# First mixer's attentions: the sign and scale folded into the queries, the two maps mixed by one operation, the output scaled on its way out of its bank by ScalarE

## The chip, the cores and the metric

The kernel runs on one core of a Trainium2 chip. The metric is the device time of one execution in microseconds (us); lower is better. All matrix products named below are in f32.

## What is computed

The whole program is two stacks of two layers on 512 tokens of width 1024. Only the first mixer of the first stack matters here. It has two attentions: A with 4 heads, each with two maps over 64-wide queries and keys and 128-wide values, and B with 8 heads of 96-wide queries and keys and 64-wide values. Cut to what is touched:

```
# attention A (diff_attention), per head and block of 128 queries
s = einsum('bhmqd,bhmkd->bhmqk', qb, k) * scale          # m = 0, 1
p = softmax(s, axis=-1)
w = p[:, :, 0] - lam * p[:, :, 1]
o = einsum('bhqk,bhke->bhqe', w, v)
...
# attention B (latent_attention), per head and block
s = (einsum(qn, k_nope) + einsum(qr, k_rope)) * scale
o = einsum('bhqk,bhke->bhqe', softmax(s), v)
```

A's output goes through an RMS norm over each head's 128 columns, and both outputs through one output projection.

## The kernel before

Each engine has its own program, and semaphores order them. `attention(name)` exists once for TensorE (PE), once for ScalarE (ACT) and once for VectorE (DVE). Each loops over blocks i of 128 queries: 16 blocks in A (4 groups, one a head, of 4 blocks) and 32 in B (8 groups). The engines are skewed against each other by whole blocks:

- PE in step i: the score products s(i) (line 1921; two maps in A, one in B), in step 2 of each group also the eight transposes that turn the next group's queries and keys (line 1906), then the four transposes t(i-2) of the exponentials (line 1936), then the four output products o(i-3) (line 1945). It goes through them in this order.
- DVE in step i: for each map a row maximum of the scores straight from the bank (line 2779) and a small product with minus the scale (line 2781), which releases the exponential; then for block i-1 the reciprocal of the sums (line 2788), in A the mixing of the two maps by two operations (lines 2792 and 2795), which releases t(i-1); then the copy of o(i-3) out of its bank (line 2805 in A, line 2808 in B, where it is also scaled by the reciprocal).
- ACT in step i: for each map the exponential with its accumulated row sum (line 1244, two records: the activation and the reading of the accumulator); in step 2 of each group the two copies of turned queries and keys out of their banks (line 1226); then the copy of the turned exponentials t(i-2) (line 1255), which releases o(i-2).

Banks of PSUM are handed out in a fixed rotation over eight, four a block in A (two scores, one t, one o), and a bank is taken again when its last reader has reported. In B's steps 6 and 10 on ACT and 8 and 12 on DVE a chunk of the output projection's weights is rounded and split (lines 1236 and 2773), in line with the attention's work. `keep_warm` issues idle products before stages in which PE would otherwise wait.

After B come the sums of squares over A's output on DVE (lines 3236 and 3238), a reciprocal root on POOL, the norm, the output projection, the layer norm, routing and 32 experts with streamed weights, and the rest of the program.

Of the kernel before, what the change touches and what calls it, by code (L numbers as in the profile page):

```python
# [7 lines left out]
ALU = mybir.AluOpType  # L8
ACT = mybir.ActivationFunctionType
# [4 lines left out]
AX_X = mybir.AxisListType.X  # L14
# [4 lines left out]
T = S // P  # L19
# [166 lines left out]
def build(nc, a, out, stages=99):  # L186
    table, where = shape_constants()
    ctx = ExitStack()
    with ctx:
# [40 lines left out]
        full = [sem(f"bank{i}_full") for i in range(N_BANKS)]  # L230
        drained = [sem(f"bank{i}_drained") for i in range(N_BANKS)]
# [5 lines left out]
        dve_done = Signal(sem("dve_done"))  # L237
# [4 lines left out]
        def signal(name):  # L242
            if name not in sig:
                sig[name] = Signal(sem(name))
            return sig[name]
# [11 lines left out]
        def ps(u):  # L257
            return psum[u.bank]
# [3 lines left out]
        U, W = {}, {}  # L262
# [227 lines left out]
        for i in range(4):  # L490
            c = plan.chunk(KD, BANK, BANK)
# [176 lines left out]
        sums, negmax, rcp = stat(64), stat(64), stat(64)  # L668
        bnst, mv, rstd = stat(T, 2, 6), stat(T, 2), stat(32)
        ssq = stat(32)  # L670
        lam = stat(8)
# [73 lines left out]
        def on(n):  # L745
# [8 lines left out]
                      v=lambda g, o, kt: E["H"][:, kt, 2 * A_QKV + 128 * g:2 * A_QKV + 128 * g + 128],  # L754
                      o=lambda g, o, t: XH[:, t, 128 * g:128 * g + 128]),
            "B": dict(groups=B_HEADS, maps=1, outs=1, rows=B_QK, scale=B_QK ** -0.5, buf=E, dv=B_V,
                      q=lambda g, t: E["QB"][:, t, g, :], k=lambda g, t: E["KC"][:, t, g, :], width=B_QK,
                      v=lambda g, o, kt: E["VB"][:, kt, g, :],
                      o=lambda g, o, t: XH[:, t, 512 + B_V * g:512 + B_V * g + B_V]),
# [310 lines left out]
        def _(act):  # L1070
# [146 lines left out]
            def attention(name, then=None):  # L1217

                c = att[name]
                u, buf, n = U[name], att[name]["buf"], att[name]["groups"] * T  # L1220

                def group(g):
                    for j in range(2):
                        v = u["qk"][g][j]
                        act.wait_ge(full[v.bank], v.n + 1)
                        act.activation(buf["QKT"][0:c["width"], g % 2, j, :], ps(v)[0:c["width"], :], ACT.Copy).then_inc(
                            drained[v.bank], 1)
                        act.wait_ge(drained[v.bank], v.n + 1)

                group(0)  # L1230
                for i in range(n + 2):
                    if then and i in (6, 10):
                        first = W[then][0]
                        ks = pieces(first)[i // 10]
                        act.wait_ge(loaded[first.slot], 16 * first.loads)
                        act.activation(one_pass(hi(first)[:, ks, :]), raw(first)[:, ks, :], ACT.Copy).then_inc(rounded[first.pair], 1)
                    if i < n:
                        for m in range(c["maps"]):
                            s = i * c["maps"] + m
                            act.wait_ge(signal("max_ready").sem, signal("max_ready").next(act))  # L1240
                            v = u["s"][i][m]
                            j = s % 64
                            act.wait_ge(full[v.bank], v.n + 1)
                            act.activation(buf["p"][i % 3][:, m, :], ps(v)[:, :], ACT.Exp, bias=negmax[:, j:j + 1], scale=c["scale"], accum_out=sums[:, j:j + 1]).then_inc(
                                drained[v.bank], 1)
                            act.wait_ge(drained[v.bank], v.n + 1)
                        if i % T == 2 and i // T + 1 < c["groups"]:
                            group(i // T + 1)
                    if i >= 2:
                        for o in range(c["outs"]):  # L1250
                            if i >= 4:
                                act.wait_ge(full[u["o"][i - 4][o].bank], u["o"][i - 4][o].n + 1)
                            v = u["t"][i - 2][o]
                            act.wait_ge(full[v.bank], v.n + 1)
                            act.activation(buf["WT"][:, (i - 2) % 2, o, :, :].rearrange("p t q -> p (t q)"), ps(v)[:, :], ACT.Copy).then_inc(
                                drained[v.bank], 1)
                            act.wait_ge(drained[v.bank], v.n + 1)
# [123 lines left out]
            n = n_dma = 0  # L1381
            for name in chan_at:
                v = a[name]
                v = v.rearrange("(r c) -> r c", c=P) if len(v.shape) == 1 else (
                    v.rearrange("l (r c) -> (l r) c", c=P) if len(v.shape) == 2 else v.rearrange("l w (r c) -> (l w r) c", c=P))
# [11 lines left out]
            for name in bc_at:  # L1397
                v = a[name]
                if len(v.shape) == 2:
                    v = v.rearrange("a b -> (a b)")  # L1400
# [30 lines left out]
            for t in range(T):  # L1431
                for j in range(2):
                    u = U["uq"][0][2 * t + j]
# [1206 lines left out]
        def _(dve):  # L2640
# [122 lines left out]
            def attention(name, then=None):  # L2763
                c = att[name]
                u, buf, n = U[name], c["buf"], c["groups"] * T

                for i in range(n + 3):
                    g, t = divmod(i, T)
                    if then and i in (8, 12):
                        first = W[then][0]  # L2770
                        ks, w = pieces(first)[i // 12], raw(first)
                        dve.wait_ge(rounded[first.pair], 2 * first.nth - 1 + i // 12)
                        dve.tensor_tensor(one_pass(w[:, ks, :]), w[:, ks, :], parts(hi(first)[:, ks, :]), ALU.subtract).then_inc(split[first.pair], 1)
                    if i < n:
                        for m in range(c["maps"]):
                            s = (i * c["maps"] + m) % 64
                            v = u["s"][i][m]
                            dve.wait_ge(full[v.bank], v.n + 1)
                            dve.tensor_reduce(negmax[:, s:s + 1], ps(v)[:, :], AX_X, ALU.max).then_inc(dve_done.sem, 1)  # L2779
                            dve.wait_ge(dve_done.sem, dve_done.next(dve))  # L2780
                            dve.tensor_scalar(negmax[:, s:s + 1], negmax[:, s:s + 1], -c["scale"], None, ALU.mult).then_inc(
                                signal("max_ready").sem, 1)
                            dve.wait_ge(signal("max_ready").sem, signal("max_ready").next(dve))
                    if 1 <= i <= n:
                        s = ((i - 1) * c["maps"]) % 64
                        for m in range(c["maps"]):
                            dve.wait_ge(drained[u["s"][i - 1][m].bank], u["s"][i - 1][m].n + 1)
                        dve.reciprocal(rcp[:, s:s + c["maps"]], sums[:, s:s + c["maps"]]).then_inc(dve_done.sem, 1)
                        dve.wait_ge(dve_done.sem, dve_done.next(dve))
                        if name == "A":  # L2790
                            p0, p1 = (buf["p"][(i - 1) % 3][:, m, :] for m in range(2))
                            dve.tensor_scalar(p1, p1, rcp[:, s + 1:s + 2], lam[:, 2:3], ALU.mult, ALU.mult).then_inc(
                                dve_done.sem, 1)
                            dve.wait_ge(dve_done.sem, dve_done.next(dve))
                            dve.scalar_tensor_tensor(p0, p0, rcp[:, s:s + 1], p1, ALU.mult, ALU.add).then_inc(
                                signal("mixed").sem, 1)
                            dve.wait_ge(signal("mixed").sem, signal("mixed").next(dve))
                    if i >= 3:
                        g2, t2 = divmod(i - 3, T)
                        for o in range(c["outs"]):  # L2800
                            v = u["o"][i - 3][o]
                            s = ((i - 3) * c["maps"] + o) % 64
                            dve.wait_ge(full[v.bank], v.n + 1)
                            if name == "A":
                                dve.tensor_copy(c["o"](g2, o, t2), ps(v)[:, 0:c["dv"]]).then_inc(drained[v.bank], 1)
                                dve.wait_ge(drained[v.bank], v.n + 1)
                            else:
                                dve.tensor_scalar(c["o"](g2, o, t2), ps(v)[:, 0:c["dv"]], rcp[:, s:s + 1], None, ALU.mult).then_inc(
                                    drained[v.bank], 1)
                                dve.wait_ge(drained[v.bank], v.n + 1)  # L2810

            def shifted(j):

# [416 lines left out]
            if on(2):  # L3230
                attention("A")
                attention("B", "even_o")

                o = XH[:, :, 0:512]
                sq = E["H"][:, :, 0:512]
                dve.tensor_tensor(sq, o, o, ALU.mult).then_inc(dve_done.sem, 1)
# [482 lines left out]
```

## Time and profile before

| what | value |
|---|---|
| time, median of 3 runs | 3312.08 us (3310.1 to 3312.66) |
| span of the profiled execution | 3301.4 us |
| busy over the span: PE, PEld, DVE, ACT, POOL | 95%, 72%, 66%, 48%, 13% |
| attention A in the profiled execution | about 150 to 215 us |
| attention B | about 215 to 307 us |

The span runs from the first to the last instruction; the time of a run takes in what lies around it. The profiled execution's own time is not among those given; its span lies 10.7 us under the median of the timed runs, and those three lie within 2.6 us of each other.

### The profile page before, as it was taken

The numbers are of one execution on the slowest core, as the hardware profiler recorded it, in microseconds if no ns is written. First come the engines' busy times: TensorE is split into PE (matmuls) and PEld (weight loads), VectorE is DVE, ScalarE is ACT, GpSimd is POOL, SyncE is SP. The second block draws the span as 40 slices with busy tenths as digits, with TensorE's granted clock in tenths as the row PEclk, the third lists the DMA queues.
The fourth block names the chain that finished last, engine by engine and source line by source line (L and its number), as shares of the span: only waits on it lengthen the run. The fifth ranks groups of instructions, "written<-read, shape, count | busy, mean of one in ns | idle before, by whom it ended". The sixth has DMA issues, their size and how long they took to land.

```text
span 3301.4 us, 39275 instructions
## 1 busy us (share of the span) xinstructions
PE 3133.6 (95%) x14815; PEld 2391.1 (72%) x14815; DVE 2171.0 (66%) x2380; ACT 1594.0 (48%) x1889; POOL 415.7 (13%) x274
## 2 busy tenths in 40 slices
PE   8879999999998989899999999998899999999998
PEld 7556667777776867577777757877788887788886
DVE  2375578888885266688888876564477745757653
ACT  2465167777774344477777754342322212722211
POOL 0000122222212000222223220010000000000000
PEclk9999999999999999999999999999999999999999
DMA  7200389999993211699999973330123223223321
GB/s 263 106 1 14 149 309 361 351 358 360 359 355 134 77 46 65 249 363 348 356 361 351 360 279 73 76 65 1 60 94 98 82 101 102 77 83 102 102 102 64
DMA packets 174479, 599.20 MB, mean 181 GB/s; under 512 B 25571, under 2 KB 74899, under 8 KB 124947
## 3 DMA queue, kind: packets, MB, share of 16 engines
q1 hardware_dynamic: 140528, 541.75, 44.9%
q0 software_dynamic: 23472, 51.42, 4.4%
q10 hardware_dynamic: 10355, 4.33, 0.5%
q8 instruction: 83, 1.36, 0.2%
q14 instruction: 41, 0.34, 0.0%
HBM read 581.17 MB, written 48.23 MB: 191 GB/s over the span
## 4 chain that ended last, share of the span: by engine, by line
PE 78%; DVE 8%; DMA 6%; ACT 4%; issue 3%; POOL 1%; DVEq 0%; SPq 0%; ACTq 0%; POOLq 0%
PE bank L1820 20%; PE bank L1822 19%; PE bank L1821 19%; DMA ring<-w_gate 3%; PE bank L1832 3%; PE bank L2368 2%; PE bank L1884 2%; PE bank L1885 2%; PE bank L2118 1%; PE bank L1827 1%; PE bank L1828 1%; DVE st L2779 1%; PE bank L1945 1%; ACT ring_rounded L1276 1%; PE bank L2149 1%
## 5 line engine op out<-in xcount | busy, mean ns | idle before, releaser
L1821 PE MATMUL bank<-ring_rounded,big_rounded 128*96 128x512 f32 (+1 forms) x1680 | 660.1, 393 | 0.0
L3019 DVE TENSOR_TENSOR ring_rounded<-ring,big_rounded 128x2048 fp32r<-128x2048 f32 x252 | 568.1, 2287 | 42.2 <-ACT big_rounded L1276 41.3
L2666 DVE TENSOR_TENSOR ring_rounded<-ring,ring_rounded 128x2048 fp32r<-128x2048 f32 (+2 forms) x124 | 273.4, 2247 | 402.0 <-ACT ring_rounded L1096 401.9
L1276 ACT ACTIVATE big_rounded<-ring 128x2048 fp32r<-128x2048 f32 x252 | 478.6, 1918 | 74.2 <-DMA ring<-w_up 56.6
L1096 ACT ACTIVATE ring_rounded<-ring 128x2048 fp32r<-128x2048 f32 (+2 forms) x124 | 226.7, 1878 | 454.9 <-DMA ring<-ffn_w_down 163.6
L1820 PE MATMUL bank<-big_rounded 128*96 128x512 f32 x992 | 395.0, 398 | 1.0 <-DVE ring_rounded L3019 0.8
L3019 DVE TENSOR_TENSOR ring_rounded<-ring,ring_rounded 128x2048 fp32r<-128x2048 f32 x128 | 292.6, 2287 | 156.4 <-ACT ring_rounded L1276 148.1
L1822 PE MATMUL bank<-big_rounded,XH_rounded 128*96 128x512 f32 x992 | 392.1, 395 | 0.0
L1821 PEld LDWEIGHTS bank<-ring_rounded,big_rounded 128*96 128x96 f32 (+1 forms) x1680 | 277.5, 165 | 105.4
L1276 ACT ACTIVATE ring_rounded<-ring 128x2048 fp32r<-128x2048 f32 x128 | 245.1, 1916 | 208.3 <-DMA ring<-w_gate 208.0
L1822 PE MATMUL bank<-ring_rounded,XH_rounded 128*96 128x512 f32 (+1 forms) x776 | 307.2, 396 | 0.0
L1820 PE MATMUL bank<-ring_rounded,big_rounded 128*96 128x512 f32 (+1 forms) x688 | 276.2, 401 | 11.8 <-DVE XH_rounded L3028 4.9
L1820 PE MATMUL bank<-XT_rounded,ring_rounded 128*128 128x512 f32 x696 | 274.1, 394 | 2.4 <-DVE big L3108 2.4
L1821 PE MATMUL bank<-XH_rounded,ring_rounded 128*128 128x512 f32 x696 | 271.6, 390 | 0.0
L1822 PE MATMUL bank<-XT_rounded,ring_rounded 128*128 128x512 f32 x696 | 271.4, 390 | 0.0
L1820 PE MATMUL bank<-ring_rounded,XT_rounded 128*128 128x512 f32 (+1 forms) x584 | 228.7, 392 | 9.4 <-DVE XH_rounded L3450 3.9
L1822 PE MATMUL bank<-ring_rounded,big_rounded 128*128 128x512 f32 (+1 forms) x608 | 235.7, 388 | 0.0
L956 POOL DMA_INDIRECT expert_rows<-big,idx x64 | 118.2, 1847 | 865.8 <-ACT big L1298 809.3
L1821 PE MATMUL bank<-ring_rounded,XT_rounded 128*128 128x512 f32 (+1 forms) x584 | 227.0, 389 | 0.0
L1822 PEld LDWEIGHTS bank<-big_rounded,XH_rounded 128*96 128x96 f32 x992 | 159.8, 161 | 70.3
L1820 PEld LDWEIGHTS bank<-big_rounded 128*96 128x96 f32 x992 | 162.2, 164 | 66.9 <-DVE ring_rounded L3019 1.7
L905 POOL TENSOR_SCALAR st<-st 128x1 f32<-128x1 f32 (+3 forms) x43 | 16.4, 382 | 1523.0 <-ACT lnp L1355 918.6
(464 smaller groups left out, 5238.1 us busy)
## 6 DMA issues: line engine op xcount, KB each, us to landing
ring<-w_up SPq DMA_DIRECT2D x128, 1024.0 KB, 7.6
ring<-w_down SPq DMA_DIRECT2D x128, 1024.0 KB, 7.8
ring<-w_gate SPq DMA_DIRECT2D x128, 1024.0 KB, 7.0
ring<-ffn_w_up SPq DMA_DIRECT2D x44, 1024.0 KB, 6.9
ring<-ffn_w_down SPq DMA_DIRECT2D x10, 2048.0 KB, 7.8
ring<-ret_gdn_w_in SPq DMA_DIRECT2D x8, 2048.0 KB, 13.3
expert_rows<-lnp POOLq DMA_DIRECT2D x1, 12288.0 KB, 40.2
ring<-odd_w_qkv SPq DMA_DIRECT2D x6, 2048.0 KB, 8.0
```

Of the source, the lines that this page charges most:

```text
L956: pool.indirect_dma_start(expert_rows, bass.IndirectOffsetOnAxis(ap=used[0:CAP, e:e + 1], axis=0), M["YE"][0:CAP, e % 2, :], None, bounds_ ...
L1096: act.activation(one_pass(hi(c)[:, ks, :]), raw(c)[:, ks, :], ACT.Copy).then_inc(rounded[c.pair], 1)
L1276: act.activation(one_pass(expert_hi(j)), expert_raw(j), ACT.Copy).then_inc(signal("half_rounded").sem, 1)
L1820: pe.matmul(dst, x_hi, y_hi, start=first, stop=False)
L1821: pe.matmul(dst, x_hi, y_lo, start=False, stop=False)
L1822: return pe.matmul(dst, x_lo, y_hi, start=False, stop=last)
L1832: return pe.matmul(dst, one_pass(x_hi), one_pass(y_lo), start=False, stop=last)
L1884: pe.matmul(dst, w, one_pass(XT[:, kk, :].rearrange("p (t c) -> p t c", t=T)), start=(kk == 0), stop=False)
L1885: pe.matmul(dst, w, x_lo, start=False, stop=False)
L2368: ins = pe.matmul(ps(u)[:, tokens(h)], lhsT[:, h, :], rhs[:, h, :], start=start and (stop or h == 0), stop=stop and (start or h == GDN_HEA ...
L2666: dve.tensor_tensor(one_pass(w), w, parts(hi(c)[:, ks, :]), ALU.subtract).then_inc(split[c.pair], 1)
L3019: dve.tensor_tensor(one_pass(expert_raw(j)), expert_raw(j), parts(expert_hi(j)), ALU.subtract).then_inc(signal("half_split").sem, 1)
```

## The change

Four edits, all in the first mixer's attentions:

1. ACT's copy of the turned queries multiplies by minus the scale (`scale=-c["scale"]` as a constant), so that the scores in the bank are already negated and scaled. DVE takes their minimum, which is what the exponential needs as its bias, and the small product of line 2781 goes. The exponential takes the constant -1 as its scale.
2. In A the two maps are mixed as e0 + (lam · sum0 / sum1) · e1: a small product on one column makes the factor, and one operation over 512 columns remains where there were two.
3. The missing factor 1/sum0 is put on A's output, as it is copied out of its bank.
4. That copy moves from DVE to ACT, `out(i)`, at the head of ACT's step i+4, ahead of that step's exponentials; ACT's loop in A has two steps more at its end. Ahead of the sums of squares DVE waits for the last four of these copies.

```diff
@@ ACT, attention
-  act.activation(buf["QKT"][...], ps(v)[...], ACT.Copy)
+  act.activation(buf["QKT"][...], ps(v)[...], ACT.Copy, scale=1.0 if j else -c["scale"])
...
+  def out(i):
+      v = u["o"][i][0]
+      act.wait_ge(full[v.bank], v.n + 1)
+      s = i * c["maps"] % 64
+      act.activation(c["o"](i // T, 0, i % T), ps(v)[:, 0:c["dv"]], ACT.Copy, scale=rcp[:, s:s + 1]).then_inc(drained[v.bank], 1)
...
-  for i in range(n + 2):
+  for i in range(n + (4 if name == "A" else 2)):
+      if name == "A" and i >= 4:
+          out(i - 4)
...
-  act.activation(buf["p"]..., ACT.Exp, bias=negmax[:, j:j + 1], scale=c["scale"], accum_out=sums[:, j:j + 1])
+  act.activation(buf["p"]..., ACT.Exp, bias=negmax[:, j:j + 1], scale=-1.0, accum_out=sums[:, j:j + 1])
...
-  if i >= 2:
+  if 2 <= i < n + 2:
@@ DVE, attention
-  dve.tensor_reduce(negmax[:, s:s + 1], ps(v)[:, :], AX_X, ALU.max)
-  dve.tensor_scalar(negmax[:, s:s + 1], negmax[:, s:s + 1], -c["scale"], None, ALU.mult)
+  dve.tensor_reduce(negmax[:, s:s + 1], ps(v)[:, :], AX_X, ALU.min)
...
-  dve.tensor_scalar(p1, p1, rcp[:, s + 1:s + 2], lam[:, 2:3], ALU.mult, ALU.mult)
-  dve.scalar_tensor_tensor(p0, p0, rcp[:, s:s + 1], p1, ALU.mult, ALU.add)
+  dve.tensor_scalar(rcp[:, s + 1:s + 2], rcp[:, s + 1:s + 2], sums[:, s:s + 1], lam[:, 2:3], ALU.mult, ALU.mult)
+  dve.scalar_tensor_tensor(p0, p1, rcp[:, s + 1:s + 2], p0, ALU.mult, ALU.add)
...
-  if i >= 3:
+  if i >= 3 and name == "B":
-      dve.tensor_copy(c["o"](g2, o, t2), ps(v)[:, 0:c["dv"]])        # A's
@@ DVE, after the attentions
+  for v in U["A"]["o"][-4:]:
+      dve.wait_ge(drained[v[0].bank], v[0].n + 1)
```

## Rows read from the trace of the kernel before

**Rows 1.** The page: the chain that ended last, by engine, as shares of the span.
```profile
PE 78%; DVE 8%; DMA 6%; ACT 4%; issue 3%; POOL 1%; DVEq 0%; SPq 0%; ACTq 0%; POOLq 0%
```

**Rows 2.** Busy time by stretch: length, busy PE, PEld, DVE, ACT, POOL, granted clock, DMA.
```profile
150.00:216.00 66.00, 51.93 (x288) 33.80 (x288) 55.06 (x128) 38.15 (x87) 0.00 (x0) 0.90 0.00 1
216.00:307.00 91.00, 82.03 (x508) 61.34 (x506) 45.60 (x130) 56.98 (x114) 0.00 (x0) 0.98 0.00 1
...
180.00:195.00 15.00, 11.98 (x75) 7.54 (x73) 13.51 (x32) 9.81 (x22) 0.00 (x0) 1.00 0.00 1
```

**Rows 3.** The timeline of one block of A on DVE, and the next block's start.
```profile
195.30 0.69 DVE L2779 TENSOR_REDUCE st<-bank 128x1 f32<-128x512 f32 x1
196.02 0.15 DVE L2781 TENSOR_SCALAR st<-st 128x1 f32<-128x1 f32 x1
196.21 0.69 DVE L2779 TENSOR_REDUCE st<-bank 128x1 f32<-128x512 f32 x1
196.26 0.69 ACT L1244 ACTIVATE big<-bank,st 128x512 f32<-128x512 f32 x1 [1.40 <-DVE st L2781]
...
197.32 0.55 DVE L2792 TENSOR_SCALAR ring<-ring,st 128x512 f32<-128x512 f32 x1
197.91 0.75 DVE L2795 SCALAR_TENSOR_TENSOR ring<-ring,st 128x512 f32<-128x512 f32 x1
198.69 0.29 DVE L2805 COPY XH<-bank 128x128 f32<-128x128 f32 x1
199.02 0.69 DVE L2779 TENSOR_REDUCE st<-bank 128x1 f32<-128x512 f32 x1
```

**Rows 4.** The timeline of ACT where it runs without a wait.
```profile
162.73 0.69 ACT L1244 ACTIVATE big<-bank,st 128x512 f32<-128x512 f32 x1
163.54 0.60 ACT L1255 ACTIVATE big<-bank 128x512 f32<-128x512 f32 x1
174.57 1.23 ACT L1226 ACTIVATE big<-bank 128x512 f32<-128x512 f32 x2
```

**Rows 5.** Groups by form, whole span: ScalarE's nearest operations to the new copy.
```profile
L1547 ACT ACTIVATE big<-bank,st 128x128 f32<-128x128 f32 x16 | 4.6, 367 | 0.1
L1517 ACT ACTIVATE big<-bank 128x128 f32<-128x128 f32 x16 | 4.4, 277 | 18.4 <-PE bank L2354 17.9
```

**Rows 6.** The timeline of PE in A; the first and the last row at the low clock.
```profile
149.98 5.49 PE L1921 MATMUL bank<-big 64*128 64x512 f32 x12 [0.98 <-ACT big L1226]
...
161.94 1.16 PE L1945 MATMUL bank<-big 128*128 128x128 f32 x8 [0.52 <-ACT big L1255]
163.03 1.13 PE L1921 MATMUL bank<-big 64*128 64x512 f32 x4
164.15 0.66 PE L1936 MATMUL bank<-const,ring 128*128 128x128 f32 x4
...
165.63 1.13 PE L1921 MATMUL bank<-big 64*128 64x512 f32 x4
...
176.48 1.95 PE L1945 MATMUL bank<-big 128*128 128x128 f32 x8 [0.52 <-ACT big L1255]
```

**Rows 7.** The chain that ended last, start and end of A, in order of time.
```profile
152.13 0.70 DVE st L2779
...
157.35 0.70 DVE st L2779
...
206.46 0.70 DVE st L2779
...
209.06 0.76 DVE ring L2795
...
215.35 0.45 PE bank L1906 x4
```

**Rows 8.** The same chain in one group of B.
```profile
268.05 0.17 DVE st L2781
```

**Rows 9.** The timeline of PE in the same group of B.
```profile
270.99 1.10 PE L1945 MATMUL bank<-lnp,big 128*128 128x64 f32 x8 [0.27 <-ACT big L1255]
```

More of the change, by code:

```diff
@@ L1225, in group @@
                         act.wait_ge(full[v.bank], v.n + 1)
-                        act.activation(buf["QKT"][0:c["width"], g % 2, j, :], ps(v)[0:c["width"], :], ACT.Copy).then_inc(
+                        act.activation(buf["QKT"][0:c["width"], g % 2, j, :], ps(v)[0:c["width"], :], ACT.Copy, scale=1.0 if j else -c["scale"]).then_inc(
                             drained[v.bank], 1)
                         act.wait_ge(drained[v.bank], v.n + 1)
+                def out(i):
[3 more added lines that the diff above has]
+                    act.activation(c["o"](i // T, 0, i % T), ps(v)[:, 0:c["dv"]], ACT.Copy, scale=rcp[:, s:s + 1]).then_inc(drained[v.bank], 1)
                 group(0)
-                for i in range(n + 2):
+                for i in range(n + (4 if name == "A" else 2)):
+                    if name == "A" and i >= 4:
+                        out(i - 4)
                     if then and i in (6, 10):
@@ L1243, in attention @@
                             act.wait_ge(full[v.bank], v.n + 1)
-                            act.activation(buf["p"][i % 3][:, m, :], ps(v)[:, :], ACT.Exp, bias=negmax[:, j:j + 1], scale=c["scale"], accum_out=sums[:, j:j + 1]).then_inc(
+                            act.activation(buf["p"][i % 3][:, m, :], ps(v)[:, :], ACT.Exp, bias=negmax[:, j:j + 1], scale=-1.0, accum_out=sums[:, j:j + 1]).then_inc(
                                 drained[v.bank], 1)
@@ L2778, in attention @@
                             dve.wait_ge(full[v.bank], v.n + 1)
[L2779 to L2782, printed above, removed]
+                            dve.tensor_reduce(negmax[:, s:s + 1], ps(v)[:, :], AX_X, ALU.min).then_inc(signal("max_ready").sem, 1)
                             dve.wait_ge(signal("max_ready").sem, signal("max_ready").next(dve))
@@ L2791, in attention @@
                             p0, p1 = (buf["p"][(i - 1) % 3][:, m, :] for m in range(2))
-                            dve.tensor_scalar(p1, p1, rcp[:, s + 1:s + 2], lam[:, 2:3], ALU.mult, ALU.mult).then_inc(
+                            dve.tensor_scalar(rcp[:, s + 1:s + 2], rcp[:, s + 1:s + 2], sums[:, s:s + 1], lam[:, 2:3], ALU.mult, ALU.mult).then_inc(
                                 dve_done.sem, 1)
                             dve.wait_ge(dve_done.sem, dve_done.next(dve))
-                            dve.scalar_tensor_tensor(p0, p0, rcp[:, s:s + 1], p1, ALU.mult, ALU.add).then_inc(
+                            dve.scalar_tensor_tensor(p0, p1, rcp[:, s + 1:s + 2], p0, ALU.mult, ALU.add).then_inc(
                                 signal("mixed").sem, 1)
                             dve.wait_ge(signal("mixed").sem, signal("mixed").next(dve))
-                    if i >= 3:
+                    if i >= 3 and name == "B":
                         g2, t2 = divmod(i - 3, T)
@@ L2803, in attention @@
                             dve.wait_ge(full[v.bank], v.n + 1)
[L2804 to L2810, printed above, removed]
+                            dve.tensor_scalar(c["o"](g2, o, t2), ps(v)[:, 0:c["dv"]], rcp[:, s:s + 1], None, ALU.mult).then_inc(
+                                drained[v.bank], 1)
+                            dve.wait_ge(drained[v.bank], v.n + 1)
             def shifted(j):
```

## The prediction

> **What bounds the kernel now.** I read the page first. Over the whole program the chain that ended last is PE's for 78% and DVE's for only 8% [rows 1]. A page-wide share says nothing about one stage, so I next read the busy times of the two attentions. In A DVE is busy 55.1 of 66 us, PE 51.9 and ACT 38.2; in B PE is busy 82.0 of 91 us, ACT 57.0 and DVE 45.6 [rows 2]. DMA moves nothing in either, so no transfer can hide or give back what happens there. The timeline of A shows who sets the pace: from one block's first maximum (199.02) back to the one before (195.30) are 3.72 us, in which DVE goes from operation to operation with some 0.03 us between them and waits for nobody, while ACT waits 1.40 us ahead of an exponential for the small product of line 2781 [rows 3]. The chain agrees: through A it is made of DVE's pieces, apart from the start, the end and one stretch near 176 us where PE ran at its low clock, so that its eight output products took 1.95 us in place of 1.16 [rows 6, 7]. In B the chain is mostly PE's, and goes through line 2781 only where a group turns [rows 8] and near the two places where weights are split.
>
> **The change part by part, in A.** A block on DVE costs today: two maxima at 0.69 and two small products at 0.15, the reciprocal, 0.55, 0.75 and 0.29, with the hand-overs 3.72 us [rows 3].
>
> - Line 2781 goes: 196.02 to 196.21 is 0.19 us, twice a block, 0.38.
> - Line 2792 (0.55, with its gap 197.91 - 197.32 = 0.59) becomes a product on one column. Its nearest row is line 2781, 0.19 with the gap; two pointer operands in place of a constant could add a little, below 0.05. Net -0.40.
> - Line 2805 leaves DVE: 199.02 - 198.69 = 0.33.
> - The remaining mixing operation has the form of line 2795 and keeps 0.75; a minimum reads as many elements as a maximum, and a constant scale on a copy or an exponential replaces a constant. I cost these at nothing; nothing hides them, it is the same instruction with another constant. If the minimum were dearer by 0.1, A would lose 0.2 a block on DVE.
>
> DVE's block is then 3.72 - 0.38 - 0.40 - 0.33 = 2.61, say 2.64 us with the pointers.
>
> DVE is then not clearly the slowest, so the other two must be counted. **ACT**: two exponentials at 0.81 start to start and the copy of line 1255 at 0.60 + 0.03 are 2.25 a block; two copies of turned queries and keys, 1.23 + 0.03, come once a group [rows 4]. The new copy is 128x128 from a bank with a pointer as its scale. The trace has that form in another stage: 0.367 us, against 0.277 for one without the pointer [rows 5]. I take 0.37 + 0.03 = 0.40, with 0.30 and 0.45 as bounds. ACT's block is 2.65, and a group 4 × 2.65 + 1.26 = 11.86. **PE** at the full clock: from one s to the next, 163.03 to 165.63, are 2.60 us, of which 1.12 are s and 1.48 are t and o; o alone is 1.09, 161.94 to 163.03 [rows 6]. The eight transposes of a group are twice the four of a t, at most 2 × 0.5, so a group is 11.4.
>
> One rule bears on the new copy. The Trainium skill, "VectorE: DVE Perf Modes", section on the TRN2 errata, prices ScalarE from PSUM at 172 cycles plus one an element at 1.2 GHz, which at 128 columns is 0.25 us, an estimate from that page. The row with a pointer has 0.367. By the page ACT's group would be 11.4 and the sum some 2 us better; the row decides. [...]
>
> Three engines now lie within 0.05 us of each other, so the loops between them count too. Following o(i-3) on PE, s(i+1), its minimum, both exponentials and the copy of t(i-1): 0.05 hand-over, 1.09 for o, 1.20 until the minimum starts (1.13 and the wait), 0.69 + 0.08, 0.81, 0.81, 0.63, together 5.36 for two blocks, 2.68 each, from [rows 3, 4, 6]. This is as long as ACT's own work. I take 2.68 and add 0.10 a block for hand-overs that don't mesh (my choice; the bounds are 0 and 0.5).
>
> The new copy stands ahead of the exponentials in ACT's order, and what is queued behind it are these exponentials, then the copy that releases the next o. It waits for o(i-4), which PE starts as ACT begins the step before and ends some 1.1 us later, so 1.5 us early; I cost that wait at nothing. If PE were late by more than this, each us of it would be a us of the block. Banks: the one of o(i-4) is taken again by a score or an o of a later step, after ACT has read it at the head of its step.
>
> The sum for A against its own rows [rows 7]:
> - Head. Blocks 0 and 1 take 152.13 (first maximum) to 157.35. PE is at the low clock and delivers the scores of three blocks in 5.49 us, 1.83 each [rows 6], so the second block's minima start near 154, and DVE ends the mixing near 156.5. Gain 0.85.
> - Blocks 2 to 14: 206.46 - 157.35 = 49.1 today. After: 13 × 2.78 + 3 × 1.26 = 39.9. Gain 9.2.
> - Tail, 206.46 to 215.35, 8.9 us. The mixing of block 14 ends 3.4 after 206.46 today and 2.64 afterwards, 0.7 to 0.8 less. What follows is PE's, from the end of the mixing at 209.82 to B's transposes at 215.35, 5.5 us for two t and three o; at the full clock they would take 2 × 1.48 + 1.0 = 4.0. Gain 0.8 to 2.3, I take 1.2. The copy of the last o then lies ahead of B's first ACT copy, but beside PE's first transposes of B (0.45 us), which cover its 0.40; without that cover it costs 0.4.
>
> A: 0.85 + 9.2 + 1.2 = 11.3 us.
>
> **In B** only line 2781 goes. On most blocks PE sets the pace and DVE waits, so it saves nothing. Where a group turns, the chain runs maximum, line 2781, exponential, two copies, copy of t, o, and PE waits 0.27 us for the last of them [rows 8, 9]: there 0.19 is gained. I count seven such places on the chain from 229 to 302 us (one a group, of which the row is the fourth), and at B's start two of the small products in a row, 0.39: 7 × 0.19 + 0.39 = 1.7 us. What is late next in those places is PE itself. Bounds 1.0 and 2.0.
>
> **Afterwards** the stages follow in series, and the loads of expert weights are released by products of the output projection, not by a clock of their own, so I pass the gain on in full.
>
> Sum 11.3 + 1.7 = 13.0 us on a span of 3301.4, so 3288.4; with the 10.7 us between span and median, 3299.1.
>
> **The rivals.**
>
> *The low clock keeps A slow.* In A the granted clock is 0.90 on average [rows 2], that is a mixture of 2.4 and 1.2 GHz. At the low level o takes 1.95 us, and from s to its maximum are 2.15 (149.98 to 152.13) [rows 6, 7]. The two-block loop is then 0.05 + 1.95 + 2.15 + 0.77 + 0.81 + 0.81 + 0.63 = 7.2, 3.6 a block: 13 × 3.6 + 3.8 = 50.6 against today's 49.1, so that A's middle gains nothing. Left are head, tail and B less 1.5, in all 1.9: 3310. Against it: PE's work in a block stays the same while the block shortens, so PE idles less than before, and from 180 to 195 us it was granted the full clock although it was busy for only 12 of 15 us [rows 2]. The Trainium skill, "TensorE: Matmul & The Clock Gate", Part 1, says the clock falls when the array idles and comes back when it is busy; by that rule the denser stage is the warmer one. Chance 0.10, most of it for a part of A, so 3303 to 3310.
>
> *Loops mesh badly or the gain is given back.* If each block loses 0.5 us, the middle gains 4.0, in all 7 to 8: 3304 to 3305; beyond that, or if routing or the first experts wait for a transfer that didn't move with the rest, 3306 to 3310. Nothing in the rows speaks for a transfer. Chance of over 3305.5 by this 0.06.
>
> *Slower.* One mechanism: B is PE's. If its later start in another phase leaves PE at 1.2 GHz there, each us of product work takes two. B has 82 us of it and now runs at 0.98 [rows 2]. The gain of 13 is used up when 13 us more of PE's work, a sixth of B, fall to the low level; a third of B gives 3312 + 14 = 3326. Against: B's own work and order don't change. Chance 0.04.
>
> *The edits do more than I say.* If the hand-overs mesh and the copy costs 0.30, DVE and PE set the pace: 13 × 2.64 + 3 × 1.0 = 37.3, a gain of 11.8, tail 2.3, B 2.0, head 0.85: 17.0, 3295. It is the lower edge of my own case.
>
> **How the numbers follow.** My forecast, 3295 to 3305, has 0.80; the low clock 0.10, lost or given back 0.06, slower 0.04. About 0.2% (6.6 us) is what a measurement of this kernel can tell, so faster means under 3305.5. Faster 0.81, same 0.14, slower 0.05. The range from 3294 to 3307 leaves out some 2 in 10.
>
> **What the profile after would show.** In A the distance between first minima should be 2.7 to 2.8 us (4.0 in the step with the group's copies), ACT nearly without waits, DVE with short waits for PE in front of the minima; the new copy at 0.37 us, the small product at 0.15 to 0.17; the same mixing operation at 0.75. A should end near 204 and B near 294 us. In B each turn of a group should be 0.19 shorter and other blocks unchanged. The prediction is wrong if the distance stays over 3.3, if ACT waits ahead of the new copy, if the clock in A lies under 0.9, or if the stages after 294 us take another time than before.

## The result

| | before | changed |
|---|---|---|
| time, median (4 runs each) | 3311.09 us (3308.45 to 3312.66) | 3287.76 us (3282.99 to 3288.43) |
| ratio, 95% interval | | 0.994 (0.9923 to 0.9956) |
| the same again later (23 and 6 runs) | 3305.09 us | 3288.54 us, ratio 0.9957 (0.9941 to 0.9973) |
| span of the profiled execution | 3301.4 us | 3286.4 us |
| own time of the profiled execution | not given | 3288.22 us |

The kernel became faster, as forecast, but both medians lie below the range (3294 to 3307), the first by 11.3 us under the 3299.1 forecast. By the medians it gained 23.3 us in the first comparison and 16.5 in the second.

Of the kernel after, the page's line on the chain, then busy time by stretch (length; busy PE, PEld, DVE, ACT, POOL; granted clock; DMA share, GB/s) for the same two windows as in [rows 2]. With the change the first window also holds some of B.

```profile
PE 80%; DVE 7%; DMA 5%; ACT 4%; issue 3%; POOL 1%; DVEq 0%; SPq 0%; ACTq 0%; POOLq 0%
```

```profile
150.00:216.00 66.00, 57.96 (x341) 38.13 (x342) 46.05 (x92) 52.52 (x121) 0.00 (x0) 0.95 0.00 1
216.00:307.00 91.00, 83.49 (x489) 60.61 (x488) 46.29 (x98) 49.08 (x98) 3.12 (x2) 0.98 0.00 1
```

In this window DVE's 55.1 us [rows 2] are 46.1 now, ACT's 38.2 are 52.5, and PE's idle time fell from 14 to 8 us; the last 12 us of it are B's now, so these are not A's sums alone. One block of A on the timeline, to be read against [rows 3]:

```profile
166.88 1.42 DVE L2787 TENSOR_REDUCE st<-bank 128x1 f32<-128x512 f32 x2
...
167.11 0.37 ACT L1234 ACTIVATE XH<-bank,st 128x128 f32<-128x128 f32 x1
...
167.61 0.69 ACT L1252 ACTIVATE ring<-bank,st 128x512 f32<-128x512 f32 x1
168.33 0.17 DVE L2793 RECIPROCAL st<-st 128x2 f32<-128x2 f32 x1
...
168.53 0.27 DVE L2797 TENSOR_SCALAR st<-st 128x1 f32<-128x1 f32 x1
168.84 0.75 DVE L2800 SCALAR_TENSOR_TENSOR big<-big,st 128x512 f32<-128x512 f32 x1
...
169.63 1.42 DVE L2787 TENSOR_REDUCE st<-bank 128x1 f32<-128x512 f32 x2
```

From one block's first minimum to the next (166.88 to 169.63) are 2.75 us where there were 3.72, and the exponential starts 0.73 after its minimum, not 0.96. The product on one column takes 0.27, dearer than the 0.15 of line 2781 and than the 0.17 that I had for it; the copy takes the 0.367 of [rows 5].

The chain that ended last, at the turn of a group of A (step 6; the minima of block 8 are at its end), shows that a whole group is not four such blocks:

```profile
169.63 0.70 DVE st L2787
170.35 0.70 DVE st L2787
...
171.19 0.55 issue
...
171.97 0.61 ACT big L1226
172.60 0.61 ACT big L1226
173.23 0.61 ACT big L1263
...
173.88 1.16 PE bank L1953 x8
175.04 1.07 PE bank L1929 x3
...
176.20 0.70 DVE st L2787
```

Two blocks at 2.75 are followed by two that take 6.57 together: ACT's two copies of turned queries and keys stand ahead of its copy of t, the next o and s wait for it, and the minima for them. The prediction had one step of 4.0 us here; there are two, of 3.40 and 3.17. A group is 12.07 us; four blocks of 3.72 were 14.9 before.

I measured A from its first row maximum to the first copy of B's queries (line 1226), B from there to the sums of squares, and the rest from there to the end of the span. The "stage" is A and B together. Of the kernel before these are 63.8 + 91.3 = 155.0 us [rows 7 for the start], of the changed one 50.6 + 88.5 = 139.0. The stage gains 16.0 us. Its start is at 153.06 in place of 152.13, and the rest is 2994.3 in place of 2994.2, so that the spans differ by 15.0.

### The profile page after: what moved, and what is told of

Same layout as the page of the kernel before. It is cut to its first block, busy times and chain, and to the rows that moved or that the text cites. A ratio compares the mean times of both kernels' runs of the same rounds, so it can differ in the third digit from the quotient of the medians.

```text
span 3286.4 us, 39211 instructions
## 1 busy us (share of the span) xinstructions
PE 3130.5 (95%) x14815; PEld 2391.3 (73%) x14815; DVE 2154.1 (66%) x2300; ACT 1599.9 (49%) x1905; POOL 391.3 (12%) x274
## 4 chain that ended last, share of the span: by engine, by line
PE 80%; DVE 7%; DMA 5%; ACT 4%; issue 3%; POOL 1%; DVEq 0%; SPq 0%; ACTq 0%; POOLq 0%
PE bank L1828 20%; PE bank L1830 20%; PE bank L1829 20%; PE bank L1840 3%; DMA ring<-w_gate 2%; PE bank L2376 2%; PE bank L1892 2%; PE bank L1893 2%; PE bank L2126 1%; PE bank L1835 1%; PE bank L1836 1%; PE bank L1953 1%; PE bank L2157 1%; PE bank L1929 1%; ACT ring_rounded L1284 1%
## 5 line engine op out<-in xcount | busy, mean ns | idle before, releaser
L1828 PE MATMUL bank<-ring_rounded,big_rounded 128*96 128x512 f32 (+1 forms) x688 | 277.1, 403 | 11.1 <-DVE XH_rounded L3029 4.7
L956 POOL DMA_INDIRECT expert_rows<-big,idx x64 | 99.2, 1550 | 888.0 <-ACT big L1306 834.5
```

What stands on the lines that cost most here:

```text
L956: pool.indirect_dma_start(expert_rows, bass.IndirectOffsetOnAxis(ap=used[0:CAP, e:e + 1], axis=0), M["YE"][0:CAP, e % 2, :], None, bounds_ ...
L1828: pe.matmul(dst, x_hi, y_hi, start=first, stop=False)
```

## The experiments

All numbers of one execution are those of its profile; the group of A is the distance between ACT's copies of queries and keys (line 1226) from one turn to the next where PE was at its full clock; the group of B is the same distance near B's end, behind the steps in which weights are split, and the text calls it a warm group. In the profile of before A's two such distances are 14.54 and, with a stretch at the low clock in it, 15.97; the 14.9 is four blocks of 3.72, and c1 and e4 show 14.88 and 14.87. In before, c1 and e8 the group of B is the last distance but one; their last is 10.7.

| kernel | A | B | stage | rest | group of A, of B | span | median | ratio (95%) |
|---|---|---|---|---|---|---|---|---|
| before | 63.8 | 91.3 | 155.0 | 2994.2 | 14.9, 10.35 | 3301.4 | | |
| c1 before | 64.3 | 91.3 | 155.7 | 3001.0 | 14.9, 10.35 | 3305.6 | 3306.96 | 0.9994 (0.9982 to 1.0006) |
| changed | 50.6 | 88.5 | 139.0 | 2994.3 | 12.07, 9.99 | 3286.4 | 3287.76 | 0.994 (0.9923 to 0.9956) |
| c2 changed | 50.3 | 89.5 | 139.8 | 2992.9 | 12.07, 9.99 | 3283.4 | 3288.54 | 0.9957 (0.9941 to 0.9973) |
| e1 | 56.2 | 89.5 | 145.7 | 3004.0 | 13.38, 9.99 | 3301.5 | 3296.74 | 0.9965 (0.995 to 0.998) |
| e2 | 55.1 | 90.7 | 145.7 | 2990.2 | 13.15, 10.35 | 3287.5 | 3295.72 | 0.9963 (0.995 to 0.9976) |
| e4 | 63.6 | 87.2 | 150.7 | 2992.6 | 14.9, 9.99 | 3294.9 | 3296.4 | 0.998 (0.9967 to 0.9992) |
| e5 | 53.6 | 89.5 | 143.1 | 3006.9 | 12.88, 9.99 | 3300.3 | 3301.24 | 0.9977 (0.9966 to 0.9988) |
| e6 | 53.1 | 88.1 | 141.2 | 2991.3 | 12.61, 10.0 | 3282.8 | 3285.51 | 0.9944 (0.9928 to 0.996) |
| e7 | 50.0 | 89.5 | 139.4 | 2994.1 | 12.0, 10.0 | 3283.9 | 3285.69 (one run) | |
| e8 | 64.2 | 96.2 | 160.4 | 2993.3 | 15.2, 10.35 | 3304.5 | 3305.19 | 0.9998 (0.9986 to 1.0011) |
| e9 | 49.3 | 83.1 | 132.4 | 3008.3 | 11.8, 9.65 | 3291.2 | 3287.28 | 0.9942 (0.9921 to 0.9963) |
| e10 | 49.1 | 83.1 | 132.1 | 2991.7 | 11.77, 9.65 | 3275.6 | 3280.32 | 0.9931 (0.9911 to 0.9951) |
| e11 | 50.7 | 84.9 | 135.6 | 2994.1 | 12.2, 9.65 | 3279.7 | 3282.36 | 0.9946 (0.9928 to 0.9964) |

The rest has the same code in all of them and takes from 2990 to 3008 us, with no relation to the edit. That is why the causes below are read from the stage and the groups. The gains by time agree with those by the stage within their intervals in all of them but e5 and e8; they are too wide to rank kernels whose stages differ by 2 or 3 us.

**c1, before, unchanged.** No edit.

> The kernel before, unchanged, once more. The profiled execution of before had a span of 3301.4 us, the timed ones 3308 to 3313 us, and after the change the span of the profiled execution lies only 1.8 us under its own time. Theory 1: the profiled execution of before was a fast one, some 7 us under the usual, and its time was lost in none of the attentions: this profile has a span of 3306 to 3311, attention stage (first row maximum to the sums of squares of A's output) 155.0 +- 1 us as before, and the excess lies in the stages with streamed weights or in the clock. Theory 2: the usual execution of before has a longer attention stage than the profiled one (160 us or more, at a lower clock), and the change gains these 8 us there. Rival to both: the span is 3301 again and the time lies around it.

Stage 155.7, rest 3001.0 against 2994.2: theory 1. The span of 3305.6 lies 1.8 us under its own time of 3307.45. The median of all 22 runs of before beside these kernels was 3307.85 (3301.27 to 3317.13).

**c2, the changed kernel again.** No edit.

> The changed kernel once more, beside many runs of before, for the ratio. The attention stage (first row maximum to the sums of squares) was 139.03 us against 155.0 and 155.7 in two profiles of before, while the rest of the program differed by up to 17 us between single profiles of all kernels, whatever the edit. Theory 1: the change gains the 16.0 to 16.6 us of the stage and nothing else: ratio 0.995 +- 0.001, some 3291 to 3292 us beside 3308. Theory 2: the 23 us of the first comparison hold, ratio 0.993 or less, and the rest of the program gains too.

Stage 139.8, ratio 0.9957, so 14 us of 3305, with 9 to 19 as its interval. This bears theory 1 (15.9 by the stage); the first ratio was a little better than that, but their intervals overlap.

**e1, edit 1 alone.**

```diff
-  dve.tensor_reduce(..., ALU.max); dve.tensor_scalar(negmax, negmax, -c["scale"], None, ALU.mult)
+  dve.tensor_reduce(..., ALU.min)          # queries copied by ACT with scale=-c["scale"], exponential with scale=-1.0
```

> Edit 1 alone, in A and B: negated and scaled queries, a minimum, no small product; the two-operation mixing and DVE's copy stay. If the gains of the edits are those of DVE's own time in A, a block goes from 3.72 to 3.34 us: A shorter by 5.5 to 6.5 us, and B by 2.8 as in the changed kernel, the attention stage 146 to 147 us in place of 155.0, the time 8 to 9 us under before. Rival: ACT and PE already limit A near 3.3 and B gains only the seven places of 0.19: stage 150 us, 5 us.

A group of A is 13.38, 4 × 3.35: DVE still paces every block, and the stage gained 9.4 us, just beyond the 8 to 9 expected; at A's end the clock stayed full here (no slice of 4 us under 0.97 from 156 to 232 us), which may be the difference. B gained 1.8 by its total, but its warm group went from 10.35 to 9.99. The median is 11.1 us under its before.

**e2, edits 2 to 4 without edit 1.** The diff of the changed kernel with the maximum, the small product and the two scales put back.

> Edits 2 to 4 without edit 1: one mixing operation, scaled copy on ACT, but maximum and small product stay. With the 0.27 us that the new small product took, DVE's block is 2.75 + 0.38 = 3.13 us: A shorter by 9 to 10 us, B unchanged, the stage 145 to 146 us and the time 9 to 10 us under before. Rival: the copy ahead of the exponentials delays them while the small product does too, and A's block is 3.3 or more: 6 us or less.

Group 13.15, stage 145.7, 9.3 us. The expected 3.13 a block (12.5 a group) was too low: like the changed kernel, it has the long turn. B's group is unchanged at 10.35. The median is 12.1 us under its before.

**e5, all but the move.**

```diff
-  ACT: out(i - 4)
+  DVE: dve.tensor_scalar(c["o"](g2, o, t2), ps(v)[:, 0:c["dv"]], rcp[:, s:s + 1], None, ALU.mult)
```

> All but the move: the mixing in one operation, 1/sum0 put on the output by DVE, which still copies it. DVE's block is 2.75 + 0.31 = 3.06 us. If DVE is still what paces A: block 3.06, A 2.5 to 4 us longer than in the changed kernel, the stage 142 to 143 us, the time 12 to 13 us under before by the stage. Rival: the group's copies on ACT and PE's order limit A, so that the move is worth nothing (stage 139 us), or ACT without the copy is freer and A gets shorter than 139.

A 53.6, so the move is worth 3.0 to 3.3 us of the 13 that A gains. The time does not bear out the stage: the median of nine runs, 3301.24, is 6.6 us under its before (interval 4 to 11), where the stage alone gained 12. The rest took 3006.9 us in its profile; why it was dear here stays open.

**e4, edit 1 in B only.** e1 with the four lines conditional on B.

> Edit 1 in B only. My prediction gave 1.7 us to B: 0.19 at one place a group. The changed kernel's B is 2.8 us shorter, edit 1 in both gave 1.9. Theory 1: there are two places a group where the small product is waited for, the maximum at the turn and the copy of t that the third output product after it waits for, so B gets 2 to 3 us shorter and A not at all (A 63.8 to 64.4). Rival: 1.7 to 1.9 is all that edit 1 gives, and the rest of B's 2.8 came from where the low clock fell.

A 63.6, B 87.2, 4.1 us less than before, and a warm group 9.99 against 10.35. Two places in a warm group it is. Eight groups at 0.36 would be 2.9 (a round count: B's first two distances got only 0.18 and 0.31 shorter); what exceeds it is mostly where the low clock fell (no stretch of it in B, groups 11.58 and 9.99 where before has 12.40 and 11.03).

**e6, two-operation mixing, the copy on ACT unscaled.**

```diff
-  dve.tensor_scalar(rcp[:, s + 1:s + 2], rcp[:, s + 1:s + 2], sums[:, s:s + 1], lam[:, 2:3], ALU.mult, ALU.mult)
-  dve.scalar_tensor_tensor(p0, p1, rcp[:, s + 1:s + 2], p0, ALU.mult, ALU.add)
+  dve.tensor_scalar(p1, p1, rcp[:, s + 1:s + 2], lam[:, 2:3], ALU.mult, ALU.mult)
+  dve.scalar_tensor_tensor(p0, p0, rcp[:, s:s + 1], p1, ALU.mult, ALU.add)
```

> The changed kernel with the old mixing in two operations, its output copied by ACT unscaled: edit 1 and the move without edits 2 and 3. DVE's block in A should be 3.72 - 0.38 - 0.33 = 3.01 us, A 54 to 55 us, the stage 142.5 to 143.5. Rival: the copy on ACT is what limits, and A is no longer than with the move and the short mixing together, 51 us, or the move alone gives nothing against edit 1 alone, 56 us.

Group 12.61, A 53.1, stage 141.2: the short mixing is worth 2.5 to 2.7 us in A, less than the 3.4 to 4.4 expected. The time can't show it: this median, 3285.51, lies 3 us under that of the changed kernel beside it (3288.54), with intervals that overlap. The copy without a pointer took 0.28 us in place of 0.367, and where the exponential behind it waits for nothing, that starts 0.17 after it:

```profile
171.72 0.28 ACT L1234 ACTIVATE XH<-bank 128x128 f32<-128x128 f32 x1
171.89 0.68 ACT L1252 ACTIVATE big<-bank,st 128x512 f32<-128x512 f32 x1
```

**e8, a filler on PE in A of the kernel before.**

```diff
   for m in range(c["maps"]):
       ...
+      if name == "A" and m == 0 and i >= 3:
+          pe.matmul(ps(v)[:, :], ident, const[:, 0:BANK], start=True, stop=True)
```

> The kernel before with one idle 128x512 product by the identity on PE ahead of each block's scores in A from the fourth block on; it goes into the bank that the scores then overwrite. PE waits over 1 us a block there, the product takes about 0.6. Theory: the fall of the granted clock in A and its tail comes from PE's idle time, and part of what the change gained in A's tail (2.2 us where I had forecast 1.2) is the clock. Then the clock from 165 us on is 1.0, the stretch near 176 us loses its 1.1 us and the tail after the last mixing goes from 5.5 to near 4.0: A shorter by 2 to 2.5 us although PE does more. Rival: the clock doesn't answer to this, A stays at 63.8 to 64.4 or gets longer by what the products delay.

The theory fell where it named a gain: A is 64.2, not shorter. The clock was 1.00 from 165 to 208 us, as expected, but so it was in c1 without a filler, and a group of A takes 15.2 in place of 14.9 by the fillers. Busy time by stretch of this kernel, columns as above, at A's end and in B:

```profile
204.00:208.00 4.00, 2.33 (x16) 1.36 (x12) 3.69 (x10) 2.42 (x7) 0.00 (x0) 1.00 0.00 0
208.00:212.00 4.00, 2.99 (x19) 2.72 (x20) 2.74 (x6) 1.32 (x3) 0.00 (x0) 0.76 0.00 0
...
224.00:236.00 12.00, 12.00 (x40) 8.50 (x40) 3.69 (x11) 5.24 (x8) 0.00 (x0) 0.50 0.00 0
```

The fillers don't reach A's end: there PE waits 2.17 us for the mixing of block 14 (no more scores to compute), and only after that does the clock fall. And in B, with no filler, 12 us passed at the low level, in which PE was busy throughout (it had waited 1.48 us just ahead of them, as it does in before, where the clock stayed at 1.00); the group with this stretch took 15.57 us for 11.22 in before, most of B's 4.9 us. So the low clock can cost this stage over 4 us in an execution, and it did so behind an A that kept PE busier. Not every execution need have it: the median, 3305.19, is that of before, 3305.09, though the profiled stage is 5.4 us longer.

**e7, the factor by another form.**

```diff
-  dve.tensor_scalar(rcp[:, s + 1:s + 2], rcp[:, s + 1:s + 2], sums[:, s:s + 1], lam[:, 2:3], ALU.mult, ALU.mult)
+  dve.scalar_tensor_tensor(rcp[:, s + 1:s + 2], rcp[:, s + 1:s + 2], lam[:, 2:3], sums[:, s:s + 1], ALU.mult, ALU.mult)
```

> The changed kernel with its one-column factor made by another form: a product with one pointer scalar and one tensor operand in place of one with two pointer scalars, which took 0.27 us where I had taken 0.19 with its gap. Expected 0.16 to 0.18, DVE's block 2.65 instead of 2.75. If DVE paces A in the two blocks of each group between which it never waits, a group goes from 12.07 to 11.8-11.9; if the way over ACT's copies sets the group, 12.07 stays. B unchanged at 9.99 a group.

The groups of the changed kernel and of this one, by form:

```profile
L2797 DVE TENSOR_SCALAR st<-st 128x1 f32<-128x1 f32 x16 | 4.4, 272 | 0.6
```

```profile
L2797 DVE SCALAR_TENSOR_TENSOR st<-st 128x1 f32<-128x1 f32 x16 | 3.5, 220 | 0.6
```

0.22, not 0.17: a pointer and a tensor operand cost 0.07 more than the 0.153 of line 2781, which has one constant, and two pointers 0.12 more. DVE's block is 2.69, a group of A 12.0. The turn sets the rest.

**e9, the group's copies last.**

```diff
   for m in range(c["maps"]): ... exponentials
-  if i % T == 2 and i // T + 1 < c["groups"]:
-      group(i // T + 1)
   if 2 <= i < n + 2: ... copy of t(i-2)
+  if i < n and i % T == 2 and i // T + 1 < c["groups"]:
+      group(i // T + 1)
```

> The changed kernel with ACT's two copies of the next group's queries and keys after the copy of t instead of ahead of it, in A and B. Theory: in both attentions the turn of a group is late because these 1.26 us stand ahead of the copy that releases the next output product. Then A's group goes from 12.07 to 11.8-11.9 (ACT's own work: 4 x 2.65 + 1.26) and B's from 9.99 to 9.7 (PE's own 4 x 2.2 + 0.9). Stage 136.5 to 138. Rival: the copies are then late themselves, and PE waits for them with the scores two blocks on: A or B no shorter.

The groups are as expected, 11.8 in A and 9.65 in B, but the stage is 132.4, below the 136.5 to 138 expected and 6.6 to 7.4 us under the changed kernel. A gained 1.0 to 1.2, B 5.4 to 6.4. Not all of B's is the edit: the changed kernel has 8 us at a granted clock of 0.79 in B (240 to 248 us) and this one has no such slice there, some 1.7 us by my estimate (0.21 of 8 us). B's first two distances between copies got shorter by 0.76 and 1.25 us, more than the 0.34 of a warm group; the expectation had not counted that, and its cause was not followed. The chain of this kernel in one group of B is PE's without a gap:

```profile
245.62 0.88 PE bank L1914 x8
246.50 0.44 PE bank L1944 x4
246.94 0.84 PE bank L1953 x8
247.78 0.91 PE bank L1929 x2
...
255.27 0.88 PE bank L1914 x8
```

0.88 + 4 × (0.44 + 0.84 + 0.91) = 9.65. At the full clock such a group can only get shorter by less work on PE. The time alone does not show this gain: the median of four runs is 3287.28, its ratio 0.9942, as the changed kernel's. The profiled execution has a rest of 3008.3, in which the first routing and experts took 657.9 us against 643.5 in the changed kernel.

**e10, both.** The edits of e7 and e9.

> The two edits together: factor by the cheaper form and the group's copies last. By DVE's own time A's group would be 4 x 2.65 = 10.6, by ACT's 11.86. If ACT's work is now the bound, it is 11.9 as with the copies last alone, and the factor's form is worth nothing; B 9.7.

The stage is 132.1, a group of A 11.77, as with the copies last alone. I had expected ACT to be the bound; the chain of one group goes over all three engines, two thirds of it on PE:

```profile
174.24 1.16 PE bank L1953 x8
175.40 1.06 PE bank L1929 x4
176.46 0.59 PE bank L1944 x4
177.04 0.89 PE bank L1953 x8
177.94 1.06 PE bank L1929 x4
179.00 1.02 PE bank L1914 x8
...
181.35 1.07 PE bank L1929 x3
...
182.51 0.70 DVE st L2787
183.23 0.70 DVE st L2787
...
185.36 0.61 ACT big L1261
...
186.01 1.16 PE bank L1953 x8
```

From o to the o a group later are 11.77 us: 8.2 in PE's products without a gap between them, then 3.6 over the minima, the exponentials and the copy of t. PE's own work would be some 10.6 a group, an estimate from the shortest of these pieces (4 × (1.06 + 0.44 + 0.89) + 1.02). So no engine's own work is the bound, but the loop between them.

The time is 3280.32, ratio 0.9931 (0.9911 to 0.9951), the lowest of all here: some 23 us under before, 8 under the changed kernel by medians that were taken at different times, 7 by the stage. The intervals of the two ratios overlap, so the step beyond the changed kernel rests on the stage.

**e11, the copies shared.**

```diff
-  if name == "A" and i >= 4:                          # ACT
+  if name == "A" and i >= 4 and i % 2 == 1:
...
-  if i >= 3 and name == "B":                          # DVE
+  if i >= 3 and (name == "B" or (i - 3) % 2 == 0):
```

> The same as before it, with A's output copies shared: DVE copies the even blocks, scaled by 1/sum0, ACT the odd ones. ACT's group is 4 x 2.25 + 2 x 0.40 + 1.26 = 11.06, DVE's 4 x 2.65 + 2 x 0.32 = 11.24, PE's 11.4. If ACT was the bound with the copies all its own, A's group comes down to 11.4-11.6, A by 1 to 1.5 us more, the stage to 135-136.5 and the time to some 19 to 20 us under before. Rival: the loops between the engines keep it at 11.8 or more.

Missed: a group of A is 12.2, longer than with all copies on ACT, and A 1.6 us longer than in e10. The stage, 135.6, lies in the forecast range only by its B, which is 1.8 longer than e10's, with a slice at 0.57 near 238 us. DVE's copy (0.36 on the chain) lies ahead of the next minima, and so ahead of the exponentials that e10 had early. ACT's own work had not been the bound. Its copy costs less than I counted, as its timeline in e9 shows, where no wait lies between:

```profile
173.08 0.37 ACT L1234 ACTIVATE XH<-bank,st 128x128 f32<-128x128 f32 x1
173.35 0.68 ACT L1252 ACTIVATE ring<-bank,st 128x512 f32<-128x512 f32 x1
```

0.27 from start to start, not 0.40: ACT's group is 4 × 2.52 + 1.26 = 11.3, under the 11.77 measured.

## Why the prediction was wrong

The direction, the mechanism and most durations held. Two steps failed: the 10.7 us that the sum added at its end, which alone puts the result outside the range, and the sizes of three terms of the stage.

**The anchor. This is the step that decided.** The last step added "the 10.7 us between span and median", as if they were a fixed part of every execution. Here span and own time of one execution differ by 1.8 us in every kernel (3286.4 and 3288.22, 3305.6 and 3307.45, 3283.4 and 3285.2). The other 8.9 were not work around the span: by this difference the profiled execution of before was one of about 3303.2 (its own time is not on record), while its timed runs happened to lie at 3308 to 3313, of a kernel whose 56 later runs have a median of 3305.5 and go from 3294 to 3317. Why those first ones all lay high stays open. My sum stood on one execution and my time on another. From 3301.4 + 1.8 it would have been 3290.2, 2.4 us from the measured 3287.76. With the stage's 16.0 exactly right and the 10.7 kept, the forecast would still have been 3296.1. That the rest of the program varies by up to 18 us was seen only afterwards; with it the range should have been wider, and its middle lower.

**The stage.** Forecast 13.0, measured 16.0 (15.9 between the repeats). By its own terms:

- Head: 0.85 forecast. The timelines have 153.06 to 157.51, 4.45 us in place of 5.22: 0.8. Held.
- Blocks 2 to 14: 9.2 forecast. From 157.51 to 196.50 are 39.0 against 49.1: 10.1. DVE's block is 2.75 and not 2.64, the factor being 0.27. It sets the pace between the turns, a little under the 2.78 of the sum, in which the 2.68 of the two-block loop were too much, as ACT's new copy costs 0.27 and not 0.40 where it isn't waited for, and the 0.10 for hand-overs was my choice. That this sum came so near is in part luck: a cheaper copy and a dearer factor offset each other. The Trainium skill, "VectorE: DVE Perf Modes", section on the TRN2 errata, had given 0.25 us as an estimate, close to these 0.27; but the same copy without a pointer has its next start 0.17 after it (e6), so the page's one figure does not hold for both forms. I decided against it by the right row for the duration (0.367) and the wrong one for the cost: the distance of two starts is what counts. The loop over two blocks was the right thing to count: at the turn of a group it is what sets the time. I had let the 1.26 us of the group's copies count once as ACT's work; they cost 1.07 (12.07 = 4 × 2.75 + 1.07).
- Tail: 1.2 forecast between 0.8 and 2.3, measured 2.2. Chain of the changed kernel:

```profile
196.50 0.70 DVE st L2787
...
199.27 0.66 PE bank L1944 x4
199.93 0.89 PE bank L1953 x8
200.82 0.44 PE bank L1944 x4
201.26 1.90 PE bank L1953 x16
203.16 0.45 PE bank L1914 x4
```

6.66 us from the last block's first minimum to B's transposes, against 8.89 [rows 7]. PE does its two t and three o in 3.9 us, the 4.0 that I had for the full clock, not 5.5. Its granted clock was 1.00 from 200 to 208 us. Ahead of it PE waits 1.20 us for the mixing of block 14, where it waited 2.17 us before the clock fell. I took the value near the wrong end. Whether the shorter wait is the cause was not isolated: e8 changed PE's load ahead of it and not the wait, and the clock fell all the same. In four profiles it fell there (before, c1, e4, e8, all with the old A on DVE); in the changed kernel, in c2, e1, e2, e5 and e6 it didn't.

- B: 1.7 forecast, 0.19 at "one place a group", measured 2.9. **Here the count of places failed, not only a size.** The totals alone would not show it: c2 and e1, with the same B and more of it at the low clock, gained 1.8. But every warm group gained 0.36, two times 0.18. The first is the maximum at the turn, as forecast. The second stands in these rows of the chain before, between one turn and the next:

```profile
273.45 0.84 PE bank L1945 x8
...
275.64 1.00 PE bank L1945 x8
276.65 0.93 PE bank L1921 x2
...
277.67 0.70 DVE st L2779
```

and in those of the changed kernel's chain at the same place:

```profile
267.30 1.10 PE bank L1953 x8
...
269.76 0.84 PE bank L1953 x8
...
271.95 0.84 PE bank L1953 x8
272.80 0.93 PE bank L1929 x2
...
273.81 0.70 DVE st L2787
```

From o at the turn to the next turn's row operation: 270.99 [rows 9] to 277.67 are 6.68, 267.30 to 273.81 are 6.51, with the same products on PE. In the kernel before, the third o took 1.00 us on the chain where the others and this kernel's third take 0.84: ACT's copy for it ended at 275.49 and it started at 275.54, so it had waited for ACT. "On most blocks PE sets the pace and DVE waits, so it saves nothing" was read from DVE's waits; PE's own small delay stood inside the duration of a product. e4 isolates it: edit 1 in B alone, 9.99 a group.

16.0 - 13.0 = 3.0 us of stage and 8.9 of anchor, less 0.9 by which this execution's stage began later, are the 11 us between forecast (3299.1) and the profiled execution's time (3288.22).

**The rivals.** The low clock did not keep A slow: 0.95 in the window where it was 0.90, and 1.00 from 165 to 208 us, where before had 0.96. (That rival's own sum was off by a little: head, tail and B less 1.5 are 2.2, not 1.9.) "Slower" by a cold B did not happen, but e8 shows that its mechanism is real, at a price of 4.4 us in the group with 12 us at half the clock. Nothing was given back: the rest is 2994.3 against 2994.2. "The edits do more than I say" came nearest, 17.0 forecast against 16.0. Of the signs of a wrong prediction none appeared in the body of A: the distance is 2.75, ACT waits ahead of the new copy only at A's end (three times, 1.2 us in all), the clock in A's window is 0.95, and the rest is unchanged.

**How the edits share the gain.** With the others in place, A loses 3.1 us without the move (e5), 2.6 without the short mixing (e6), and 4.6 without edit 1 (e2); edit 1 alone gives 7.6 to 8.1 of A's 13.2. Some 2.6 of the 13.2 are the low clock of before (1.1 in the group near 176 us, 1.5 in the tail), and part of it is in those 7.6 to 8.1: sixteen blocks at 0.37 less are 5.9. Taken out one at a time they add up to 10.3 of the 13.2. My reading is that the last ones meet the turn of the group, which no edit touched and which e9 then made shorter; this split was not tested further.

## What to carry to other kernels

Add a predicted difference to the own time of the execution that was profiled, not to the median of others, and ask first how much the untouched part varies. When an engine at the bound is relieved, walk the loop between engines once around the irregular step too (here the turn of a group): an operation that is not needed for two blocks stood ahead of one that was needed at once, and moving it by three lines took 7 us off the stage, of which some 1.7 may be the clock, beside the 16 of the change itself. A producer's delay of 0.16 us showed here in no wait, but in one product of several equal ones that took longer than its neighbours.

## What the runs showed of the hardware

- The 128x128 copy on ScalarE with a pointer lasts 0.367 us, but the next exponential starts 0.27 after it if it isn't held by a wait (e9); without the pointer it lasts 0.28, and the next starts 0.17 after it (e6).
- A product on one column took 0.153 us with a constant, 0.22 with one pointer and a tensor operand, 0.27 with two pointers.
- The granted clock was 0.50 for 12 us in which PE was busy without a gap (e8), and two profiles of one kernel have a lower clock in different places (c2: near 230 and 242 us, the first profile of the changed kernel: near 244). What starts it is open.
- The two stages of experts, with the routing ahead, took from 641 to 658 us each in kernels whose code there is the same; they make most of the differences in the rest. ACT waits there for the gate weights' transfers, 106.3 us in total in the first of them in the changed kernel and 110.5 in e9, whose stage of experts is 14 us longer; so what makes up these 14 us is not shown.
